# Six modulation blocks as row sums on VectorE, low products last, and another order of loads in a fused encoder layer

## What is computed

```python
c_act = jax.nn.silu(c)
mod = c_act @ ada_w[l] + ada_b[l]
sh1, sc1, gt1, sh2, sc2, gt2 = [m[:, None, :] for m in jnp.split(mod, N_MOD, axis=-1)]
h = rms_norm(x, norm1_g[l]) * (1.0 + sc1) + sh1
proj = h @ w_in[l]
...
o_a = gla_mixer(q, k, v, g_out, gk_low, ...)
o_b = ssd_mixer(z, xbc, dt_raw, ...)
merged = gate_a * (o_a @ w_oa[l]) + gate_b * (o_b @ w_ob[l])
x = x + gt1 * (merged @ w_out[l])
h = rms_norm(x, norm2_g[l]) * (1.0 + sc2) + sh2
x = x + gt2 * hier_moe(h, ...)      # 32 experts, top 2 of 8 in one of 4 groups
```

## Time and profile before

| | |
|---|---|
| median of 3 runs | 701.45 us (700.1 to 701.8) |
| the profiled execution | 700.86 us, span 699.0 us, mean granted clock 0.991 |
| busy in the span | TensorE 669.4 us (96%), VectorE 420.1 (60%), ScalarE 264.8 (38%), GpSimd 71.4 (10%) |
| transfers | 201.23 MB, mean 288 GB/s |
| chain that ended last | TensorE 77%, VectorE 9%, DMA 6%, ScalarE 3% |

### The profile page before, as it was taken

The page is one execution under the profiler, slowest core; times in us unless marked ns, Lnnn a source line. Parts: engine busy times, 40 slices in busy tenths (PEclk is TensorE's granted clock), DMA queues, the critical chain, the costliest instruction groups (busy, mean ns, idle before and its releaser), DMA issues.

```text
span 699.0 us, 12784 instructions
## 1 busy us (share of the span) xinstructions
PE 669.4 (96%) x5402; PEld 538.5 (77%) x5402; DVE 420.1 (60%) x710; ACT 264.8 (38%) x373; POOL 71.4 (10%) x70
## 2 busy tenths in 40 slices
PE   8999999999999999999998999899999999999893
PEld 8999999998777777999988997675666666665441
DVE  4656788987866789977786678644333122221226
ACT  3346545557763624335552332312131121221003
POOL 0001000000003614300000000001112111111111
PEclk9999999999999999999999999999999999999998
DMA  8987764455343443346639976999999999999992
GB/s 363 423 353 243 298 248 175 130 177 191 121 157 130 161 142 121 122 140 253 241 108 397 410 280 249 423 421 418 419 397 418 421 421 421 419 418 418 420 355 95
DMA packets 31195, 201.23 MB, mean 288 GB/s; under 512 B 5047, under 2 KB 5431, under 8 KB 7970
## 3 DMA queue, kind: packets, MB, share of 16 engines
q1 hardware_dynamic: 27378, 193.27, 70.7%
q0 software_dynamic: 3760, 7.14, 2.8%
HBM read 195.35 MB, written 10.75 MB: 295 GB/s over the span
## 4 chain that ended last, share of the span: by engine, by line
PE 77%; DVE 9%; DMA 6%; ACT 3%; issue 2%; SPq 2%; DVEq 0%; POOL 0%; ACTq 0%; POOLq 0%
PE ps L1571 75%; DMA ring<-in_expert_pieces 4%; DVE ring_rounded L934 2%; DMA ring<-in_pieces 2%; ACT ring_rounded L644 2%; SPq L461 1%; PE ps L1988 1%; PE ps L1692 1%; DVE r_ct L1209 1%; DVE r_v L1209 1%; DVE r_xs_rounded L1239 1%; ACT sq L760 1%; DVE g_sb L1142 0%; DVE r_kq L1173 0%; DVE newton L920 0%
## 5 line engine op out<-in xcount | busy, mean ns | idle before, releaser
L934 DVE TENSOR_TENSOR ring_rounded<-ring,ring_rounded 128x2048 fp32r<-128x2048 f32 x60 | 136.8, 2291 | 38.8 <-ACT ring_rounded L644 38.5
L1571 PE MATMUL ps<-hT_rounded,ring_rounded 128*128 128x256 f32 x832 | 150.1, 286 | 1.1 <-ACT hT_rounded L658 1.1
L1571 PEld LDWEIGHTS ps<-hT_rounded,ring_rounded 128*128 128x128 f32 x832 | 129.2, 193 | 5.1 <-issue 3.9
L644 ACT CAST ring_rounded<-ring 128x2048 fp32r<-128x2048 f32 x60 | 114.1, 1906 | 34.4 <-PE ps L1571 18.8
L1571 PE MATMUL ps<-ring_rounded,hT_rounded 128*128 128x512 f32 x352 | 109.7, 393 | 0.9 <-DVE ring_rounded L934 0.9
L1571 PE MATMUL ps<-x_sb_rounded,ring_rounded 128*128 128x256 f32 x416 | 109.8, 284 | 0.0
L1571 PEld LDWEIGHTS ps<-x_sb_rounded,ring_rounded 128*128 128x128 f32 x416 | 77.3, 193 | 0.9 <-issue 0.2
L1571 PEld LDWEIGHTS ps<-ring_rounded,hT_rounded 128*128 128x128 f32 x352 | 64.3, 188 | 14.8 <-issue 1.4
L858 ACT ACTIVATE sq<-ps 128x128 f32<-128x128 f32 x32 | 8.9, 277 | 142.6 <-PE ps L1571 142.6
L1454 DVE TENSOR_TENSOR r_st<-ps,r_kq 128x512 f32<-128x512 f32 x32 | 22.1, 692 | 65.0 <-PE ps L1571 65.0
L603 POOL DMA_INDIRECT y_rows<-r_st,r_btm x29 | 28.5, 984 | 311.4 <-DVE r_st L1454 298.6
(11 more groups left out here) (336 smaller groups left out, 1002.9 us busy)
## 6 DMA issues: line engine op xcount, KB each, us to landing
ring<-in_pieces SPq DMA_DIRECT2D x66, 1024.0 KB, 5.0
ring<-in_expert_pieces SPq DMA_DIRECT2D x48, 1024.0 KB, 17.5
r_z<-in_expert_pieces SPq DMA_DIRECT2D x12, 1024.0 KB, 13.3
r_xs<-in_expert_pieces SPq DMA_DIRECT2D x12, 1024.0 KB, 12.5
r_v<-in_pieces SPq DMA_DIRECT2D x6, 1024.0 KB, 7.2
r_ct<-in_pieces SPq DMA_DIRECT2D x6, 1024.0 KB, 5.6
g_sb<-in_expert_pieces SPq DMA_DIRECT2D x6, 1024.0 KB, 17.2
r_st<-in_expert_pieces SPq DMA_DIRECT2D x6, 1024.0 KB, 17.9
```

The lines of the kernel that those rows point to most:

```text
L644: nc.scalar.copy(high_of(p_), slot_of(p_)).then_inc(hi_ok, 1)
L934: nc.vector.tensor_tensor(low_of(p_), slot_of(p_), high_of(p_).bitcast(F32), ALU.subtract).then_inc(lo_ok, 1)
L1571: return nc.tensor.matmul(o, l, r, start=start, stop=stop)
```

## The change

It does four things. (1) Modulation blocks 4 and 5 leave `PIECES` and TensorE and become row blocks too: `rows_out(4)` stands ahead of the scaling of `z_tm`, `rows_out(5)` behind it, then bias and diagonals; the two `gtb` products move behind `oa` block 1, their copies ahead of `rows_out(7)`. (2) `c_rows` moves to `r_q`; its load waits for the last `z` product (`y_done`) and its Silu stands ahead of the second half of `gate` 2. `c_half` is filled after all row sums. (3) In both kinds of unit the products with the high part of a piece come first and wait for it alone (`high_ready`), those with the low part last (`low_ready`). (4) SP's loads from `gate` on stand in another order, and row blocks 8 and 9 are summed behind the first and the second half of `ob` block 0.

```diff
-ADA_AFTER = {("xbc", i): 3 + i for i in range(1, 3)}
-ADA_ORDER = [("quarter", q) for q in range(QUARTERS)] + [("ada", i) for i in range(4, 6)]
+ADA_ORDER = [("quarter", q) for q in range(QUARTERS)]
...
-ROW_PIECES = [("row", i, h, 0) for i in range(6, 10) for h in range(2)]
-ROWS_AT = {("oa", 1, 1): 7, ("ob", 0, 1): 8, ("ob", 1, 1): 9}
+ROW_PIECES = [("row", i, h, 0) for i in range(4, 10) for h in range(2)]
+ROWS_AT = {("oa", 1, 1): 7, ("ob", 0, 0): 8, ("ob", 0, 1): 9}
...
-        c_rows = r_pv[:, 0:2, :].rearrange("p a b -> p (a b)")
+        c_rows = view(r_q, "p d -> p d")
...
                 if n >= LOADS and PIECES[n - LOADS] == ("gate", 2, 0, 0):
                     mix_wait(sp, ("diag", 3, 1))
-                    load_rows(6)
-                if n >= LOADS and PIECES[n - LOADS] == ("oa", 1, 0, 0):
-                    mix_wait(sp, ("obT", 7))
-                    load_rows(7)
-                    load_moe(0)
-                    load_moe(1)
-                    for h in range(2):
-                        sp.dma_start(gt2_two[h * W:(h + 1) * W], gate_bias[h].partition_broadcast(W)).then_inc(s_wr, 16)
+                    load_rows(4)
...
                     for h in range(2):
                         unit_taken(sp, ("oa", 1), h)
+                    sp.dma_start(r_btm[:, 0:KD * 36 + 36], router_w).then_inc(s_wr, 16)
                     load_moe(3)
-                if n >= LOADS and PIECES[n - LOADS] in (("ob", 0, 0, 1), ("ob", 1, 0, 1)):
-                    piece_used(sp, PIECES[n - LOADS])
-                    load_rows(8 + PIECES[n - LOADS][1])
                 load_piece(n, p_)
+                if n >= LOADS and PIECES[n - LOADS] == ("gate", 3, 0, 0):
+                    load_rows(5)
+                if n >= LOADS and PIECES[n - LOADS] == ("oa", 0, 0, 0):
+                    load_rows(6)
+                if n >= LOADS and PIECES[n - LOADS] == ("oa", 0, 1, 0):
+                    mix_wait(sp, ("obT", 7))
+                    load_moe(0)
+                    load_moe(1)
+                if n >= LOADS and PIECES[n - LOADS] == ("oa", 1, 0, 0):
+                    load_rows(7)
+                if n >= LOADS and PIECES[n - LOADS] == ("ob", 0, 0, 1):
+                    load_rows(8)
+                if n >= LOADS and PIECES[n - LOADS] == ("ob", 0, 1, 1):
+                    load_rows(9)
+                if n >= LOADS and PIECES[n - LOADS] == ("ob", 1, 0, 1):
+                    sp.wait_ge(start_row_read, 4 + len(ROW_PIECES))
+                    for p_q in GATE_ROWS[:2]:
+                        sp.dma_start(slot_of(p_q), piece_src(p_q)).then_inc(s_gate, 16)
...
-            mix_wait(pool, ("gtb", 0, 1))
+            pool.wait_ge(y_done, 4 * TT)
             pool.dma_start(c_rows, c_row.partition_broadcast(P)).then_inc(s_crow_fng, 16)
...
-            modulation_rows(0)
+            split_to(SPLIT_AT["gate", 3, 1, 0] + 1)
+            rows_out(4)
             dve.wait_ge(y_sq, TT * SG)
             rstd(sss[:, 0], 256)
...
+            split_to(SPLIT_AT["oa", 0, 1, 0] + 1)
+            rows_out(5)
+            dve.wait_ge(start_row_read, 4 + 4)
+            link(nc.vector.tensor_tensor(mod[:, 16:24], mod[:, 16:24], col("ada_b", 16, 8), ALU.add))
...
-                    for a in range(2):
-                        for r in range(n_r):
-                            w = parts((*u, half, r))
+                    for r in range(n_r):
+                        p_ = (*u, half, r)
+                        w = high_ready(p_)
+                        for a in range(2):
                             for k in range(KD):
-                                ins = split_product(bank[:, a * T:(a + 1) * T], [v[:, k, a * P:(a + 1) * P] for v in w],
...
+                                for part in src:
+                                    mm(bank[:, a * T:(a + 1) * T], w[:, k, a * P:(a + 1) * P], part[:, r * KD + k],
+                                       r == 0 and a == 0 and k == 0 and part is src[0], False)
+                        w = low_ready(p_)
+                        for a in range(2):
+                            for k in range(KD):
+                                ins = mm(bank[:, a * T:(a + 1) * T], w[:, k, a * P:(a + 1) * P], src[0][:, r * KD + k], False,
+                                         r == n_r - 1 and a == 1 and k == KD - 1)
+                        ins.then_inc(done if r == n_r - 1 else ob_read, 1)
```

More of the change, by code:

```diff
@@ L1268, in _ @@
                         if (name, i, h) in ROWS_AT:
-                            if (name, i) == ("ob", 1):
-                                before((("out", 0), 0))
+                            if name == "ob":
+                                split_to(SPLIT_AT["ob", 1, h, 0] + 1)
+                            else:
+                                for n_h in range(2):
+                                    bank = mix_wait(dve, ("gtb", n_h))
+                                    nc.vector.tensor_copy(gt1b[:, n_h * CW:(n_h + 1) * CW], bank[:]).then_inc(mix_used(("gtb", n_h)), 1)
                             rows_out(ROWS_AT[name, i, h])
@@ L1661, in token_major, with with_high @@
                 for half in range(2):
-                    w = [v.rearrange("p a b -> p (a b)").rearrange("p (k n) -> p k n", n=CW) for v in parts((*u, half, 0))]
-                    for t in range(TT):
-                        bank, done = bank_of(u, t)
+                    p_ = (*u, half, 0)
+                    by_rows = lambda v: v.rearrange("p a b -> p (a b)").rearrange("p (k n) -> p k n", n=CW)
+                    def with_high(t):
+                        w = by_rows(high_ready(p_))
+                        bank = bank_of(u, t)[0]
                         for kh in range(KD // 2):
```

113 lines of the change are left out of this document (44 added, 69 removed).

## The result

Five runs of the changed kernel took 695.38 us in the median (693.1 to 698.4), beside 700.99 us for the kernel before on the same chip: a ratio of 0.9926, with a 95% interval of 0.9898 to 0.9954. It is faster, by 5.2 to 5.6 us (by the ratio, by the medians) where 13.5 were forecast, and the time lies above the range of 684.5 to 693.0. The profiled execution of the change is the one of 695.38 us, with a span of 693.6 us against 699.0.

The account below looks back on a forecast made before the run. TensorE was taken to bound the trunk, with an expert stream slower than its reader, whose starting lead decides the end waits. Terms -4.2 - 0.9 - 4.9 - 2.4 + 1.5 - 2.6 = -13.5 on 701.45 gave 687.9 us, range 684.5 to 693.

Parts of the forecast that it names:

- Term 1: Convolution: modulation blocks 4 and 5 leave TensorE, 2 x (13.59 - 11.51) = -4.2 us; their VectorE transposes and loads free nothing binding.
- signs of being wrong: VectorE waiting over 8 us for a row block, low-part waits over 1 us in ob, expert-piece waits 2.6 us or more.
- signs of being right: Convolution blocks at 11.5 us, no low-part or x_sb waits, ob clock 1.00, obT wait 1-3 us, expert-piece waits under 1 us.
- Term 2: High products first: the low part is wanted 3.8 us later, so TensorE's wait at 244.37 goes, -0.9 us.
- Term 3: Load order around oa and ob: the late ob piece lands earlier; its wait and slow clock go, -3.2 - 1.7 = -4.9 us.
- Term 4: Row block 9 is summed an ob half earlier, so the wait at 438.46 for x_sb goes: -2.4 us.
- term 6: Row blocks 6 to 9: VectorE stands before loads twice, low parts in ob block 1 have 4 us or more cover: 0.
- Term 5: Eight added row sums on VectorE make TensorE wait 1.5 us more in obT; bounds 0 and 5 us.
- The slower rival: Row-block load-and-sum chain on two buffers sets the pace if each load takes 14.5 us: 709 us, chance 0.07.
- Term 7: ScalarE: extra table loads of 1.28 us around c's Silu and before the first expert's fit idle time: 0, at most 1.3.
- Term 8: Expert stream: its lead over TensorE grows by 3 us, removing the six expert-piece waits: -2.6 us, bounds 0 and -2.6.
- The rival in which this term is 0: Expert stream takes the bound: slots come free later, its saving is 0 or turns to +2; 690.5 to 692.5 us, chance 0.20.

Follow-up runs that it names:

- experiment 5: Kernel before with the new product order (low weights last) alone; modulation blocks, loads and banks as before: 694.84 us, ratio 0.9932.
- experiment 6: experiment 1's kernel with the old product functions, so moved blocks and loads alone: 698.3 us, ratio 0.9983 to before.
- experiment 1: Changed kernel with the PSUM banks of the small product and first four turned convolution blocks set as before the change: 691.05 us, ratio 0.9883 to before.
- experiment 3: Changed kernel with ScalarE's high parts of the first two out pieces ahead of its last copies of m: 694.9 us, ratio 0.9932 to before.
- experiment 4: Changed kernel with row block 9 summed on VectorE one half of ob later, loads unmoved: 695.53 us, ratio 0.9947 to before.
- experiment 8: experiment 1's kernel with only an eighth of expert pieces 16 and 17 (early) loaded: 690.78 us, ratio 0.9865 to before.
- experiment 9: experiment 1's kernel with only an eighth of expert pieces 60 and 61 (late) loaded: 685.98 us, ratio 0.9807 to before.
- the change again: The changed kernel, unaltered, timed in a second set of runs: 694.04 us, ratio 0.9922 to before.
- experiment 10: experiment 1's kernel with the gate sum and two diagonal products on VectorE moved behind the obT copies: 688.05 us, ratio 0.9842 to before.
- experiment 2: Kernel before with only the small product's bank moved from 6 to 4, which the first half of q uses: 705.58 us, ratio 1.0085.
- experiment 7: experiment 1's kernel in the new order, but high products wait until the piece's low part is there too: 694.98 us, ratio 0.9937 to before.
- experiment 11: Changed kernel with the edits of experiment 1, experiment 3, experiment 4 and experiment 10 together: 688.26 us, ratio 0.9847 to before.

## Why the prediction was wrong

*Term 1, the modulation blocks (-4.2).* The blocks did get shorter by that much (11.51 us each). The step that failed is the sentence behind it, that what goes with them "frees nothing that binds": I looked for what the two steps used, and not for what hung on their places in a list. The shifted bank cost 2.04 us of wait and at least 1.7 us of clock. Undone, it gives back 3.0 (by the ratios) to 4.3 us (by the medians), the largest part of the miss of 7.5 us. None of the listed signs of being wrong came, and of the signs of being right only one stayed away, waits for expert pieces under 1 us: no sign looked at where the blocks begin, only at how long they take.

*Term 2 (-0.9)* came: no wait at 244. *Term 3 (-4.9)* came in size, with the wrong reason. It was the order of the products, not that of the loads (experiments 5 and 6). The clock was 1.00 in `ob`, as said.

*Term 4 (-2.4)* came: no wait for `x_sb`. But at the start of `out` 1.50 + 0.66 us took its place in the profiled execution. The step at fault is term 6's cover of 4 us or more. It was counted for low parts queued on VectorE, and held for these in all of `ob`. Not counted was that ScalarE waits for VectorE to copy m, and that a high part is queued behind that. The larger of the two waits is not there in every execution.

*Term 5 (+1.5 in `obT`).* The wait grew by 1.74 us, from 0.61 to 2.35. Right in size by the trace. But the other profiles with a wait of 2.3 to 2.7 us here (experiments 1, 3, 4, 8, 9 and the change again) all have a low clock around it, as shown with experiment 10, and that was not in the term. The change's own profile has none there: the wait brings the low clock in six profiles of seven. Removing 1.4 us of VectorE's work was worth 2.6 to 3.0 us.

*Term 6, VectorE before the row blocks.* It waited 0.83, 1.34, 4.27 and 0.66 us for blocks 5, 7, 8 and 9, and none of it reached 8. Block 8's row:

```profile
391.39 1.23 DVE L1193 SCALAR_TENSOR_TENSOR r_ct<-r_ct,r_kq 128x1024 f32<-128x1024 f32 x1 [4.27 <-DMA r_v<-in_pieces]
```

The forecast had it landed at 390.4 in the axis of before. The slower rival, loads of 14.5 us, did not come: 9.9 us was the longest in the chain.

*Term 7, the table loads (0).* Right, and the trace decides against the longer price again. ScalarE's rows, the load and then the activation:

```profile
321.56 1.28 ACT L784 ACT_TABLE_LOAD   x1
322.85 1.06 ACT L784 ACTIVATE r_kq<-r_kq 128x1024 f32<-128x1024 f32 x1
323.93 1.28 ACT L787 ACT_TABLE_LOAD   x1
325.23 0.60 ACT L787 ACTIVATE r_st<-ps 128x512 f32<-128x512 f32 x1
```

1.29 and 1.30 us from the load to the next activation, twice. The Trainium skill, ScalarE: Activation LUTs, section What ACT_TABLE_LOAD costs, has 2.66 us for a switch; nothing here shows the second half of it, neither behind the load nor ahead of it, where a cast ends 0.02 us before the first load.

*Term 8, the expert stream (-2.6).* This is the second large miss. The waits went from 2.6 to 2.3 us. I had let the stream's earlier start at 410 us count as lead, less 7 us of idle. But a slot comes free only when TensorE has read it, and from 450 us on every load waits for a slot. SP's queue shows it, first before, then after:

```profile
464.51 2.06 SPq L461 DMA_DIRECT2D r_z<-in_expert_pieces  x2
```

```profile
459.85 2.06 SPq L451 DMA_DIRECT2D r_z<-in_expert_pieces  x2
```

The same loads go out 4.66 us earlier, and TensorE starts the experts 4.67 us earlier: against its reader, the stream has gained nothing. What it had in hand was lost as idle DMA, most of it at 455 to 460 (share 0.45, where the kernel before had 1.01). From the first expert product to the last product the change needs 222.7 us and the kernel before 223.5: 0.8 us of the 2.6 came. The rival in which this term is 0 had 0.20 of the chance, at 690.5 to 692.5; with the bank it would have been 3 to 4 us more, which no case held.

One reading was loose without touching the sum: the DMA rates of the earlier trace rows are 243 to 423 GB/s in the first six slices, and 108 to 253 only from the seventh to the 21st.

## What to carry to other kernels

Where buffers or banks are dealt out by position in a list, taking out an entry moves its neighbours: print the assignment of both versions beside each other before costing the removal at its own duration. A wait on TensorE can cost twice its length or more, because of the low clock around it: 1.4 us less of work for VectorE ahead of such a wait gave 2.6 to 3.0 us, and a 2.0 us wait made 6.0. It need not: waits of 2.35 and 2.39 us (`obT` in the change, `x_sb` in the kernel before) stand in a clock of 1.00. A stream with a fixed number of slots can't be helped by an earlier start once its slots are full; only fewer bytes in the part where it sets the pace help: 4.4 us less of transfer gave 4.8 us in the medians, and 2.4 to 3.9 in the traces.

## What the runs showed that was not expected

The stretch of low clock at 60 us of the kernel before (0.66 over five us) comes with no named wait ahead of it, and not in every execution. Of the fourteen profiles, five have the wait of 2.04 us for the copy of q. All five show the low clock, and from 55 to 75 us lose 3.4 (the change), 3.5 (the change again) and 5.1 us (experiments 2, 3 and 4) to it. Nine have no wait there. Three of them lose 1.7 us all the same (before and experiments 1 and 5), and in six the clock stays at 1.00 (experiments 6 to 11), although the work of those up to there is the same as in experiment 1. So the wait does not make the stretch by itself; with it the stretch always came and was longer. Executions of one kernel can differ by 1.7 us for this alone, and a single profile may show or hide a microsecond or two that belongs to no edit.
